# Routing joined to the memory attention's output projection with its logits as rows, and the first context attention joined to the neighbourhood stage

## The reference, cut to what matters

```python
def context_attention(q, k, v):
    s = jnp.einsum('bqhd,bkhd->bhqk', q * HEAD_DIM ** -0.5, k).astype(jnp.float32)
    p = jax.nn.softmax(s, axis=-1).astype(v.dtype)
    return jnp.einsum('bhqk,bkhd->bqhd', p, v)
```

```python
g_logits = (t @ w_rg).astype(jnp.float32) + b_rg.astype(jnp.float32)
e_logits = ((t @ w_re).astype(jnp.float32) + b_re.astype(jnp.float32)).reshape(-1, N_GROUPS, EXPERTS_PER_GROUP)
e_in = jnp.take_along_axis(e_logits, g_idx[:, :, None], axis=1)[:, 0]
top_v, top_i = lax.top_k(e_in, TOP_K_IN_GROUP)
p_exp = jax.nn.softmax(top_v, axis=-1)
```

## Time and profile before

| | us |
|---|---|
| median of 3 runs (2703.9 to 2713.04) | 2707.59 |
| the profiled execution | 2712.28 |
| its span, first to last instruction | 2710.5 |
| TensorE busy (15076 records) | 2526.5 (93%) |
| VectorE busy | 1351.4 (50%) |
| ScalarE busy | 867.9 (32%) |
| GpSimd busy | 284.9 (11%) |
| mean granted TensorE clock | 0.972 |

### The profile page before, as it was taken

The page is one execution under the profiler, slowest core; times in us unless marked ns, Lnnn a source line. Parts: engine busy times, 40 slices in busy tenths (PEclk is TensorE's granted clock), DMA queues, the critical chain, the costliest instruction groups (busy, mean ns, idle before and its releaser), DMA issues. The chain is left out here.

```text
span 2710.5 us, 35809 instructions
## 1 busy us (share of the span) xinstructions
PE 2526.5 (93%) x15076; PEld 1959.7 (72%) x15076; DVE 1351.4 (50%) x2187; ACT 867.9 (32%) x1398; POOL 284.9 (11%) x231
## 2 busy tenths in 40 slices
PE   7999989999999899999899999998979999998976
PEld 5887557888888788897669999774744578773322
DVE  3323544566666412523656777437566855523213
ACT  3224424333332311424444433324332743320001
POOL 0501420000000000301500000000032020011112
PEclk9999979999999999999999999999999999988999
DMA  6113730111111112123612222420200114348997
GB/s 246 57 61 120 251 110 32 63 63 63 63 63 48 43 65 79 63 78 134 214 47 78 94 94 80 159 94 16 80 25 9 47 63 140 125 200 348 420 422 299
DMA packets 56625, 322.25 MB, mean 119 GB/s; under 512 B 8014, under 2 KB 14286, under 8 KB 24526
## 3 DMA queue, kind: packets, MB, share of 16 engines
q1 hardware_dynamic: 44510, 299.11, 30.0%
q0 software_dynamic: 5696, 12.59, 1.2%
q10 hardware_dynamic: 6256, 8.23, 0.9%
HBM read 315.71 MB, written 12.58 MB: 121 GB/s over the span
## 5 line engine op out<-in xcount | busy, mean ns | idle before, releaser
L977 PE MATMUL ps<-work_rounded,ring_rounded 128*128 128x512 f32 (+1 forms) x2016 | 533.4, 352 | 12.9 <-DVE ring_rounded L882 4.9
L977 PE MATMUL ps<-xn_rounded,ring_rounded 128*128 128x512 f32 (+2 forms) x2304 | 540.7, 347 | 0.0
L2060 PE MATMUL ps<-xn_rounded,ring_rounded 128*128 128x258 f32 (+2 forms) x2816 | 533.7, 312 | 0.0
L2060 PEld LDWEIGHTS ps<-xn_rounded,ring_rounded 128*128 128x128 f32 x2816 | 413.7, 190 | 31.0
L977 PEld LDWEIGHTS ps<-xn_rounded,ring_rounded 128*128 128x128 f32 x2304 | 371.7, 190 | 57.4 <-issue 0.2
L977 PEld LDWEIGHTS ps<-work_rounded,ring_rounded 128*128 128x128 f32 x2016 | 333.4, 190 | 71.6 <-DVE work_rounded L397 7.6
L977 PE MATMUL ps<-big_rounded,ring_rounded 128*128 128x512 f32 (+1 forms) x1200 | 320.0, 358 | 19.4 <-DVE ring_rounded L882 14.6
L882 DVE TENSOR_TENSOR ring_rounded<-ring,ring_rounded 128x2048 fp32r<-128x2048 f32 (+3 forms) x106 | 191.8, 1812 | 268.1 <-ACT ring_rounded L847 268.1
L2060 PE MATMUL ps<-work_rounded,ring_rounded 128*128 128x256 f32 (+1 forms) x1232 | 279.8, 309 | 5.7 <-DVE ring_rounded L2111 4.2
L847 ACT ACTIVATE ring_rounded<-ring 128x2048 fp32r<-128x2048 f32 (+3 forms) x106 | 160.6, 1518 | 313.7 <-PE ps L977 287.9
L977 PEld LDWEIGHTS ps<-big_rounded,ring_rounded 128*128 128x128 f32 x1200 | 198.6, 192 | 59.5 <-DVE ring_rounded L882 16.7
(11 more groups left out here) (421 smaller groups left out, 3164.4 us busy)
## 6 DMA issues: line engine op xcount, KB each, us to landing
ring<-in_stream SPq DMA_DIRECT2D x141, 1024.0 KB, 4.8
big<-in_experts SPq DMA_DIRECT2D x44, 1024.0 KB, 25.9
ring<-in_stream SPq DMA_DIRECT2D x32, 704.0 KB, 4.1
ring<-in_experts SPq DMA_DIRECT2D x22, 1024.0 KB, 26.7
xn<-in_experts SPq DMA_DIRECT2D x15, 1024.0 KB, 28.7
work<-in_experts SPq DMA_DIRECT2D x15, 1024.0 KB, 29.0
big<-in_first_modulation SPq DMA_DIRECT2D x8, 1024.0 KB, 14.1
work<-in_bias ACTq DMA_DIRECT2D x20, 256.0 KB, 4.4
```

Of the source, the lines that this page charges most:

```text
L977: mm = pe.matmul(out[:, a - u.first:b - u.first], lhs, rhs, start=j == 0 and n == 0 and not u.onto, stop=j == terms - 1 and n == len(passe ...
L2060: mm = pe.matmul(out[:, a:b], ws[:, k, :], x[k][:, a - base:b - base], start=k == 0 and n == 0, stop=k == KT - 1 and n == 2)
```

## The change

1. `neighbourhood` and `context_attention` share one block. The attention gets other banks (2, 3, 6, 7 for scores, 0 and 1 for transposes, 4 for results), and a function `arrive` that makes TensorE wait, at its first use of each, for what the neighbourhood stage still does with it (its turned tiles copied, its pool scaled, its last result stored, its modulation finished).
2. The memory attention's output projection and the routing share one block. The logits are made as rows: 8 products with 36 weight columns as the loaded operand and 512 tokens moving; ScalarE copies the 36x512 result, four transposes bring it to tokens on partitions. The scaling of the weights moves into the projection; the last square is added on VectorE; the square root's table is loaded inside the projection; ScalarE's first exponential moves between the token copies; fillers stand before the rank products (3) and the slot products (2). SP starts the expert loads when the projection's products are done, the last (down weights of expert 5) when the squares are summed.
3. The experts' stage begins with four fillers instead of three.

The core of the diff, with its definitions and spacing cut:

```diff
@@ -1069,9 +1073,10 @@
...
         stat = self.small[:, 0:16].rearrange("p (a b) -> p a b", a=4)
-        spsum = [self.ps[:, i * 512:i * 512 + width] for i in range(4)]
-        tpsum = [self.bank(b, width) for b in ((4, 7) if paired else (4,))]
-        opsum = [self.bank(b) for b in ((6,) if paired else (5, 6, 7))]
+        score_banks, turn_banks, out_banks = banks or ((0, 1, 2, 3), (4, 7) if paired else (4,), (6,) if paired else (5, 6, 7))
+        spsum = [self.bank(b, width) for b in score_banks]
+        tpsum = [self.bank(b, width) for b in turn_banks]
+        opsum = [self.bank(b) for b in out_banks]
@@ -1104,6 +1109,8 @@
...
                         pe.wait_ge(exped.sem, exped.at(u - 3))
+                    else:
+                        arrive(pe, "scores", u)
@@ -1113,6 +1120,8 @@
...
                         pe.wait_ge(copied.sem, copied.at(u - len(tpsum) + 1))
+                    else:
+                        arrive(pe, "turned", u)
@@ -1122,6 +1131,8 @@
...
                     h, i = head_and_tile(members[0])
+                    if g == 0:
+                        arrive(pe, "out", 0)
@@ -1139,6 +1150,8 @@
...
                     for n in share[u][0:1]:
+                        if n == 0:
+                            arrive(pe, "modulation", 0)
@@ -1611,7 +1625,8 @@
...
                     for a, b in pool_runs:
-                        dve.tensor_scalar(px[:, n, a:b], pooled[n][:, a:b], self.v(("pool_scale", l), n), None, ALU.mult)
+                        ins = dve.tensor_scalar(px[:, n, a:b], pooled[n][:, a:b], self.v(("pool_scale", l), n), None, ALU.mult)
+                    ins.then_inc(pool_evicted.up(), 1)
@@ -1655,8 +1670,23 @@
...
         px, va = self.px, self.va
+        copied, pool_evicted, stored, stepped = self.sig("turned_copied"), self.sig("pool_evicted"), self.sig("stored"), self.sig("vector_step")
...
+        def arrive(pe, area, n):
...
+            if area == "scores" and n < 2:
+                pe.wait_ge(copied.sem, copied.at(n - 1))
+            elif area == "scores":
+                pe.wait_ge(pool_evicted.sem, pool_evicted.at(-1))
+            elif area == "turned":
+                pe.wait_ge(pool_evicted.sem, pool_evicted.at(0))
+            elif area == "out":
+                pe.wait_ge(stored.sem, stored.at(0))
+            else:
+                pe.wait_ge(stepped.sem, stepped.at(0))
@@ -1665,7 +1695,7 @@
...
             modulation=ModulationProducts(self, MOD_CONTEXT, MOD_SECOND - MOD_CONTEXT, self.bank(5), tiles_in(256, self.work[:, 9216:9728])),
-            paired=Paired(lambda p: px[:, NAQ + p, S:T]))
+            paired=Paired(lambda p: px[:, NAQ + p, S:T]), banks=((2, 3, 6, 7), (0, 1), (4,)), arrive=arrive)
@@ -1952,13 +1982,13 @@
...
-    def output_projection(self, src, segments, residual, prefetch=None, add=None, gpsimd=None, next_sources=None, tiles_ahead=0, rooms=None):
+    def output_projection(self, src, segments, residual, prefetch=None, add=None, gpsimd=None, next_sources=None, tiles_ahead=0, rooms=None, after=None):
...
         units = [Unit([m // 2], halves(m), range(KT), P, width) for m in range(KT)]
-        next_high, after = self.sig("next_high"), None
+        next_high = self.sig("next_high")
@@ -2191,8 +2221,8 @@
...
             self.neighbourhood(l, need_ctx)
-        if need_ctx:
-            self.context_attention()
+            if need_ctx:
+                self.context_attention()
@@ -2800,8 +2830,8 @@
...
         self.squares = self.work[:, 7168:7680]
-        passing = tiles_in(S, self.work[:, 0:3 * S])
-        squared, added, landed = self.sig("squared"), self.sig("squares_added"), self.sig("inputs_landed")
+        passing = self.passing = tiles_in(S, self.work[:, 8192:8192 + 3 * S])
+        squared, added, landed, scaled = self.sig("squared"), self.sig("squares_added"), self.sig("inputs_landed"), self.sig("scaled")
@@ -2814,15 +2844,28 @@
...
             act.activation(self.squares if m == 0 else passing[(m - 1) % 3], self.x[:, m, :], ACT.Square).then_inc(squared.up(), 1)
+            if m == KT - 2:
...
+                act.activation(self.small[:, 124:125], self.ones[:, 0:1], ACT.Sqrt)
...
+        def scale_weights(dve, m):
...
+            if m == 3:
+                gain = self.v("ffn_g", 0, KT).unsqueeze(2).to_broadcast([P, KT, 36])
+                dve.wait_ge(landed.sem, landed.at(48))
+                dve.tensor_tensor(self.route_weights, self.route_weights, gain, ALU.mult).then_inc(scaled.up(), 1)
...
             pool.wait_ge(squared.sem, squared.at(1))
-            for m in range(1, KT):
+            for m in range(1, KT - 1):
...
-        self.output_projection(lambda k: o[:, k, :], [(0, S, None)], lambda m: self.x[:, m, :], prefetch=prefetch, add=square, gpsimd=add_squares,
-                               tiles_ahead=6, rooms=self.output_high)
+        with self.without_border():
+            self.output_projection(lambda k: o[:, k, :], [(0, S, None)], lambda m: self.x[:, m, :], prefetch=prefetch, add=square, gpsimd=add_squares,
+                                   tiles_ahead=6, rooms=self.output_high, after=scale_weights)
+            self.route()
@@ -2859,19 +2902,28 @@
...
         chose, ranked, valued, tabled = self.sig("combined"), self.sig("ranked"), self.sig("valued"), self.sig("tabled")
+        last_square = self.passing[(KT - 2) % 3]
...
         rank = lambda n: self.rank[:, 8 - n:8].unsqueeze(1).to_broadcast([P, 4, n])
-        log_ps, sum_ps, rank_ps, table_ps = self.bank(0, 144), self.bank(1, 4), self.bank(2, 160), self.bank(3, 64)
+        log_ps, sum_ps, rank_ps, table_ps = self.bank(0, 144), self.bank(3, 4), self.bank(0, 160), self.bank(2, 64)
+        rows_ps, logit_rows = self.bank(1, S, 36), self.work[0:36, 3584:4096]
+        projected, evicted, squared, added = self.done, self.sig("taken_by_vector"), self.sig("squared"), self.sig("squares_added")
+        totalled, rows_copied = self.sig("squares_totalled"), self.sig("logit_rows_copied")
...
             def _(pe):
+                pe.wait_ge(scaled.sem, scaled.at(0))
+                for k in range(KT):
+                    pe.wait_ge(evicted.sem, evicted.at(k + 1 - KT))
+                    mm = pe.matmul(rows_ps, w[:, k, :], x[:, k, :], start=k == 0, stop=k == KT - 1)
+                mm.then_inc(done.up(), 1)
+                pe.wait_ge(totalled.sem, totalled.at(1))
                 for t in range(4):
-                    mm = pe.matmul(sum_ps[:, t:t + 1], self.squares[:, t * P:(t + 1) * P], self.ones[:, 0:1], start=True, stop=True)
+                    mm = pe.matmul(sum_ps[:, t:t + 1], self.squares[:, t * P:(t + 1) * P], self.ones[:, 0:1], start=t == 0, stop=t == 3)
                 mm.then_inc(summed.up(), 1)
-                pe.wait_ge(scaled.sem, scaled.at(1))
+                pe.wait_ge(rows_copied.sem, rows_copied.at(1))
                 for t in range(4):
-                    for k in range(KT):
-                        mm = pe.matmul(log_ps[:, t * 36:(t + 1) * 36], x[:, k, t * P:(t + 1) * P], w[:, k, :], start=k == 0, stop=k == KT - 1)
+                    mm = pe.transpose(log_ps[:, t * 36:(t + 1) * 36], logit_rows[:, t * P:(t + 1) * P], self.ident[0:36, 0:36])
@@ -2881,12 +2933,14 @@
...
+                self.keep_multiplying(pe, self.bank(1), 3)
...
                 mm.then_inc(ranked.up(), 1)
+                self.keep_multiplying(pe, self.bank(1), 2)
@@ -2897,15 +2951,18 @@
...
             def _(act):
+                act.wait_ge(done.sem, done.at(1))
+                act.activation(logit_rows, rows_ps, ACT.Copy).then_inc(rows_copied.up(), 1)
...
                 for t in range(4):
+                    if t == 2:
+                        act.wait_ge(ready.sem, ready.at(1))
+                        act.activation(ex, ex, ACT.Exp).then_inc(exped.up(), 1)
...
                 act.dma_start(self.tokens_dram.rearrange("(t p) c -> p t c", p=P), tokens).then_inc(stored.up(16), 16)
-                act.wait_ge(ready.sem, ready.at(1))
-                act.activation(ex, ex, ACT.Exp).then_inc(exped.up(), 1)
@@ -2922,11 +2979,12 @@
...
-                gain = self.v("ffn_g", 0, KT).unsqueeze(2).to_broadcast([P, KT, 36])
-                dve.tensor_tensor(w, w, gain, ALU.mult).then_inc(scaled.up(), 1)
+                dve.wait_ge(squared.sem, squared.at(0))
+                dve.wait_ge(added.sem, added.at(0))
+                dve.tensor_tensor(self.squares, self.squares, last_square, ALU.add).then_inc(totalled.up(), 1)
...
                 do(dve.reciprocal(rstd, rstd))
-                dve.wait_ge(done.sem, done.at(1))
+                dve.wait_ge(done.sem, done.at(2))
@@ -3002,7 +3060,10 @@
...
             def _(sp):
+                sp.wait_ge(projected.sem, projected.at(0))
                 self.sparse.load_beside_routing(sp)
+                sp.wait_ge(totalled.sem, totalled.at(1))
+                self.sparse.load_dn(sp, 5)
@@ -3347,7 +3407,6 @@
...
         self.load_dn(sp, 3)
-        self.load_dn(sp, 5)
```

(2 more changed lines are left out.)

5 lines of the change are left out of this document (3 added, 2 removed).

## The result

| | median | runs | lowest to highest |
|---|---|---|---|
| before, timed beside it | 2704.59 us | 19 | 2691.52 to 2717.81 |
| changed | 2686.64 us | 19 | 2681.97 to 2706.22 |

The ratio is 0.994, with a 95% interval of 0.9923 to 0.9958: faster by more than the 0.3% that a measurement tells, and 18 us in the medians. The 19 times of the changed kernel lie in two groups: 15 from 2682 to 2691.2 us, 4 from 2702.1 to 2706.2. The profiled execution is one of the four: 2706.22 us (span 2704.4), against 2712.28 for the profiled execution of before. So the pair of profiles differs by 6.1 us and the medians by 18; most of this study is about the other 12.

The account below looks back on a forecast made before the run. TensorE, busy 93% of the span, bounds the kernel, with half-clock stretches in the context attention and routing. 6.6 + 0.9 - 0.85 + 1.1 = 7.8 us off the 2707.6 median gives 2699.8; own range 2695 to 2705, stated range 2680 to 2706.

Parts of the forecast that it names:

- Logits as rows, 6.6 us: Routing: logits as 16 records in 6.9 us let VectorE start on them (time L) 6.6 us earlier.
- about 9 us after the last add: Routing, sign to look for: VectorE's logits come about 9 us after the projection's last add, not 16.
- Rival C: Routing: clock falls halfway through the row products and fillers run at half clock; 3.4 us slower, 2711, chance 0.05.
- From L to the gather, 0.9 us gained: Routing, from VectorE's start on the logits (L) to GpSimd's gather: 0.9 us gained, bounds -1.5 to 2.0.
- ready between L+9.5 and L+10.7: Routing: when the rank products would be ready, counted from VectorE's start on the logits (L).
- The case set beside it: Routing: the two fillers before the slot table, if at the half clock, could cost 1 us.
- The store of the token rows: Routing: the gather's other condition, landing about 2440.5, nearly level with the slots; cuts off gains beyond 7.5 us.
- The fourth filler, 0.85 us lost: Ahead of the experts: a fourth filler on the path loses 0.85 us, nothing if TensorE is still at full clock.
- The joined start, 1.1 us: Context attention: without the border the first turn comes at 329.9 instead of 330.98, 1.1 us earlier.
- rival B: Context attention: the clock survives the joined start, saving 15 to 17 us there; 2684 in all, chance 0.30.
- if it falls, the rest runs as now: Context attention: should the clock fall at the joined start, the remainder of the stage is unchanged.
- The test that I set for being wrong: Wrong if the stretch 330 to 374 shrinks by over 3 us, or the gather is under 6 us earlier.

Follow-up runs that it names:

- sixth experiment: Changed kernel with the context attention's idle start filled, but logits made by the 32 products of before, in the joined stage; one run, 2691.93 us.
- fifth experiment: Changed kernel with the context attention's idle start filled and no fillers ahead of ranks and slots; median 2686.64 us, ratio 0.9944.
- ninth experiment: Kernel of the fifth experiment with three fillers ahead of the experts and two expert loads held until the token rows are stored; 2686.97 us, ratio 0.9945.
- seventh experiment: Kernel of the third experiment with three fillers instead of four ahead of the experts; one run, 2686.99 us.
- second profile: The changed kernel run once more, unedited, to profile another execution; one run, 2691.28 us.
- fourth experiment: Kernel before, border kept, with fillers around the border ahead of the context attention; median 2695.96 us, ratio 0.9963.
- third experiment: Changed kernel with five small fillers in TensorE's 2.35 us wait at the joined context attention's start; median 2686.64 us, ratio 0.9933.
- second experiment: Kernel before with only the routing part: projection joined, logits as rows, all fillers, context attention separate; median 2702.69 us, ratio 0.9987.
- eighth experiment: Kernel before with four dense products ahead of the context attention's second turn; median 2698.47 us, ratio 0.9991.

## Why the prediction was right or wrong

**Logits as rows, 6.6 us: right.** 6.5 measured; 16 records at full clock, 7.06 us against 6.9. The sign "about 9 us after the last add" doesn't fit its own sum, which gives 10.0; 10.13 came. The split (join 2.0, rows 4.5) is from the sixth experiment. Rival C needed the clock to fall in the row products and to be down when the token transposes end. It did neither: the clock reads 1.00 in 2421 to 2422 and in 2426 to 2427. In the latter only transposes had run since 2423.28; the Trainium skill ("TensorE: Matmul & The Clock Gate", Part 4: PE-mode transpose) says that these don't engage the full clock, and this trace disagrees a second time.

**From L to the gather, 0.9 us gained: wrong in sign, inside its bounds.** 1.05 us were lost (L to the gather 16.85 before, 17.90 now). The exponentials' wait went and the first fillers ended in time, both as written. The step that failed is "ready between L+9.5 and L+10.7": the ranks came at L+11.6. They start 0.24 us later against L and take 4.45 us instead of 3.84, since the clock falls 2 us into them; without any fillers they take 4.26 (fifth experiment). The case set beside it, that the two fillers before the table run at the half clock and cost 1 us, is what happened: slots at L+16.7 with them, at L+15.75 without. I had priced the fillers and not asked whether dense products in front can hold the clock through 28 small ones behind. With some half a microsecond of idle between them they don't; in the one profile with none (sixth experiment) the clock held through the ranks.

**The store of the token rows: right in kind.** It was named as the condition next in line, and in the fifth experiment it is. Its landing was put at 2440.5; issued at 2429.74 and 9.5 us under way it was at 2439.2 on a time axis that lies 2.8 us earlier (last add 2413.34 against 2416.11): 25.9 us after the last add against 24.4 as written, and 1.0 ahead of the slots. The ninth experiment shows the cause of its 9.5 us: loads of another queue on the same engines, which is what the Trainium skill ("Trainium Kernel Development and Optimization", Key Constraints) says of them; here the trace agrees, 6.5 us without those loads against 9.5 to 10.6 beside them.

**The fourth filler, 0.85 us lost: right for the filler, not for the stretch.** Taken out of the changed kernel with its start filled it gives 0.97 (seventh experiment). But from the gather to the experts' first product it was 8.98 us before and is 9.08 now, only 0.1 more. Three fillers took 5.15 us before, at 0.50 nearly to their end; the four of now take 5.30, since the clock is up when they begin (0.90 in 2442 to 2443) and back in 2446 to 2447. The term of the sum that compares the two kernels is 0.1, not 0.85.

**The joined start, 1.1 us: right.** 1.18, with one idle stretch of 2.35 us where I had written 2.5, and the clock at 0.50 behind it.

**The time: right in sign, wrong by its own test.** Profile against profile the forecast was 7.8; the four terms measured give 6.5 (6.5, -1.05, -0.1, 1.2) and the profiles differ by 6.1, the 1.95 us of the second part being the largest miss. But the median is 13 us below the 2699.8 forecast, 18 us under before where 7.8 were forecast. It lies near rival B's 2684, by a mechanism that B did not have; that the stated range holds it was luck, since the range reached so low only for B's sake. B said that the clock survives; in all three profiles of the joined start without fillers it falls. The step that failed is "if it falls, the rest runs as now", and before it, reading the 40 us of one trace as what this mix of instructions does. The same instructions gave falls of 10 and of 37 us. The test that I set for being wrong is met: the gather is 5.4 us earlier, not 6, and in the second profile the stage is 14.3 us shorter (47.90 to 33.55). In the first profile it is 2.0 us shorter, within the 3 allowed.

**Where the 18 us are.** Routing 5.3 (three profiles agree: 37.11, 36.95 and 37.14 against 42.45), joined start 1.2. The clock's part is an estimate from means. By the fourth experiment before loses 10.2 us on average, plus the 1.7 by which its fillers lengthen the start, 11.9. The changed kernel still loses 4.5 (its mean against the third experiment's), so 7.4 come from there. The sum is 13.9, against 15.8 between the means of the 19 runs each (2706.2 and 2690.3). It is rough: the mean of before alone moves by 4 us from session to session. The medians differ by more, since before's falls between its two groups of times and the changed kernel's into its lower one.

**What stays open:** why an unedited execution takes the long fall or the short one, and why the changed kernel takes the long one less often (4 of 19 above 2702; of the 33 runs of before in the first session 17 are above 2705). The kernel of the second experiment, with its border kept, took a low mean clock (0.973 to 0.975) in 7 of 12 runs, so the routing isn't what makes it rarer. It isn't shown to be the join: that alone left 3 of 12 runs above 2710 and gave an interval that includes no change. Nor is it shown how long an idle stretch must be: at 320.6 us of the kernel before TensorE idles 0.60 us ahead of small products and the clock stays at 1.00, and no run varied the length at the joined start. What is shown is that filling the idle start removes both falls.

## What to carry to other kernels

Before taking a low-clock stretch of one trace as a fixed cost or as fixed cover, profile the unedited kernel again: its length can differ almost fourfold between executions, and by more than the edit is worth. Where a stage begins with a wait of some 2 us on TensorE and goes on in small products, fill that wait up to the release of the next real instruction and no further; it cost nothing here and removed the fall of the clock, long and short. Fillers that ended half a microsecond ahead of a short run of narrow products bought nothing. And when a chain is shortened, look at which other condition of its last instruction is next: here a DMA that other loads had slowed by 3 to 4 us stood 1 us behind.

## What was new in the hardware

- At 100% busy the clock went with the number of moving columns: 36 loaded columns against 512 moving held 1.00 for 7 us, 128 loaded against 36 moving, begun 1.4 us behind dense work, lost it 2.6 us in (sixth experiment). The 28 rank products of 32 moving columns lost it 2 us in with 0.55 us of idle ahead, and kept it for their 3.21 us with none.
- Once down, the clock stayed down for 10 to 40 us of unbroken work in small tiles. With four dense products (5.67 us) put into that stretch no run of 12 was among the long ones, where 8 of 23 were (eighth experiment).
- Two executions of one program, same order and same waits, differed by 14.9 us; 12.4 of them lie in one stage and go with its granted clock.
